# A modulation row computed with the weight tile as the stationary operand

## The reference

```
mod = silu(c) @ mod_w[i] + mod_b[i]          # c: (1, 2048), mod_w[i]: (2048, 12288)
sh_m, sc_m, g_m, sh_f, sc_f, g_f = split(mod, 6)
h = rmsnorm(x, norm_mix_g[i]) * (1 + sc_m) + sh_m
q = h @ w_in[:, 0:1024]; ...                 # the first products of layer 0
```

## Time and profile before

| | us |
|---|---|
| runs, median (3 runs) | 2393.55 (2393.1 to 2397.02) |
| profiled execution | 2393.17 |
| its span, first to last instruction | 2391.2 |
| TensorE busy | 2308.2 (97%) |
| DVE busy | 1847.2 (77%) |
| ACT busy | 1096.9 (46%) |
| mean granted TensorE clock | 0.982 |

### The profile page before, as it was taken

The page is one execution under the profiler, slowest core; times in us unless marked ns, Lnnn a source line. Parts: engine busy times, 40 slices in busy tenths (PEclk is TensorE's granted clock), DMA queues, the critical chain, the costliest instruction groups (busy, mean ns, idle before and its releaser), DMA issues.

```text
span 2391.2 us, 26862 instructions
## 1 busy us (share of the span) xinstructions
PE 2308.2 (97%) x10800; PEld 1870.2 (78%) x10800; DVE 1847.2 (77%) x1748; ACT 1096.9 (46%) x1192; POOL 126.6 (5%) x145
## 2 busy tenths in 40 slices
PE   5999999999999999999998999999999999999998
PEld 2478887778887888878887788877887888878886
DVE  5868997887998888888888777887777556564565
ACT  2244443544554354533554555435555345444454
POOL 0021740010000000000000000000000000000000
PEclk8999999999999999999999999999999999999999
DMA  9958789787997998889889475696776555555554
GB/s 363 383 198 293 250 300 351 250 315 268 348 325 275 359 336 304 291 303 370 323 281 330 130 224 187 253 340 218 274 270 223 193 194 178 190 177 193 193 180 154
DMA packets 259807, 632.89 MB, mean 265 GB/s; under 512 B 23505, under 2 KB 32745, under 8 KB 233978
## 3 DMA queue, kind: packets, MB, share of 16 engines
q1 hardware_dynamic: 258050, 625.90, 73.8%
q10 hardware_dynamic: 1656, 5.60, 0.6%
HBM read 629.36 MB, written 2.10 MB: 264 GB/s over the span
## 4 chain that ended last, share of the span: by engine, by line
PE 80%; DVE 8%; DMA 5%; issue 3%; ACT 2%; SPq 1%; POOL 1%; DVEq 0%; POOLq 0%; ACTq 0%
PE gm L1911 22%; PE gm L1912 22%; PE gm L1918 22%; PE tp L1954 2%; PE gm L1903 2%; DMA mods<-in_mod_w_dram 2%; PE gm L1905 2%; PE gm L1904 2%; DVE w_lo L1213 1%; DVE acc L1230 1%; DVE conv L1659 1%; DMA raw<-in_ffn_w_down_dram 1%; ACT w_hi L764 1%; PE ms L2064 1%; DMA raw<-in_gla_w_in_dram 1%
## 5 line engine op out<-in xcount | busy, mean ns | idle before, releaser
L1213 DVE TENSOR_TENSOR w_lo<-raw,w_hi 128x2048 fp32r<-128x2048 f32 (+1 forms) x378 | 851.9, 2255 | 330.2 <-ACT w_hi L764 328.5
L764 ACT ACTIVATE w_hi<-raw 128x2048 fp32r<-128x2048 f32 (+1 forms) x378 | 703.8, 1864 | 695.5 <-DMA raw<-in_ffn_w_up_dram 242.2
L1911 PE MATMUL gm<-w_hi,h_hi 128*128 128x512 f32 x1816 | 720.7, 397 | 1.6 <-DVE h_lo L1327 1.6
L1912 PE MATMUL gm<-w_hi,h_lo 128*128 128x512 f32 x1816 | 708.1, 390 | 0.0
L1918 PE MATMUL gm<-w_lo,h_hi 128*128 128x512 f32 x1816 | 448.7, 389 | 0.0
L1230 DVE SCALAR_TENSOR_TENSOR acc<-mods,c_col,acc 128x2048 f32<-128x2048 f32 x180 | 422.7, 2349 | 5.3 <-DMA mods<-in_mod_w_dram 4.8
L1911 PEld LDWEIGHTS gm<-w_hi,h_hi 128*128 128x128 f32 x1816 | 341.2, 188 | 77.9 <-issue 4.7
L1918 PEld LDWEIGHTS gm<-w_lo,h_hi 128*128 128x128 f32 x1816 | 340.9, 188 | 70.7
L1912 PEld LDWEIGHTS gm<-w_hi,h_lo 128*128 128x128 f32 x1816 | 341.3, 188 | 69.9 <-issue 1.7
L1911 PE MATMUL gm<-w_hi,a_hi 128*128 128x512 f32 x692 | 275.1, 398 | 11.6 <-DVE a_lo L1682 8.1
L1912 PE MATMUL gm<-w_hi,a_lo 128*128 128x512 f32 x692 | 271.2, 392 | 0.0
(11 more groups left out here) (267 smaller groups left out, 2155.0 us busy)
## 6 DMA issues: line engine op xcount, KB each, us to landing
raw<-in_ffn_w_up_dram SPq DMA_DIRECT2D x176, 1024.0 KB, 5.1
mods<-in_mod_w_dram SPq DMA_DIRECT2D x170, 1024.0 KB, 7.1
raw<-in_ffn_w_down_dram SPq DMA_DIRECT2D x64, 1024.0 KB, 5.1
raw<-in_gla_w_in_dram SPq DMA_DIRECT2D x48, 1024.0 KB, 5.2
mods<-in_kv_mod_w_dram SPq DMA_DIRECT2D x32, 1024.0 KB, 7.0
raw<-in_ffn_w_down_dram SPq DMA_DIRECT2D x32, 768.0 KB, 4.4
raw<-in_gla_w_o_dram SPq DMA_DIRECT2D x16, 1024.0 KB, 7.1
raw<-in_mla_w_o_dram SPq DMA_DIRECT2D x16, 1024.0 KB, 5.6
```

What stands on the lines that cost most here:

```text
L764: act.activation(w_hi[:, k % RAW, 0:words], raw[:, k % RAW, 0:words], ACT.Copy).then_inc(hi_made, 1)
L1213: dve.tensor_tensor(w_lo[:, k % RAW, 0:words], raw[:, k % RAW, 0:words], w_hi[:, k % RAW, 0:words].bitcast(F32), ALU.subtract).then_inc(lo ...
L1911: pe.matmul(o, hi_s[:, kt, tok], wh[:, j, :], start=kt == 0, stop=False)
L1912: pe.matmul(o, lo_s[:, kt, tok], wh[:, j, :], start=False, stop=False)
```

## The change

The tiles of scale that go to TensorE become the stationary operand, one 128x128 block at a time, and c the moving one, a single column. A tile takes 16 such matmuls in place of 4. The result comes out as columns, and adds up in PSUM in the same columns as the sums over `acc`: columns 0 to 3 of `ms` are shift, 4 to 7 scale. A matmul of the identity with the bias columns opens the group (`pre_bias`), so the bias is in it too. A round now needs one fill of `ms` in place of three. DVE's add of the row (L1477), its memset in round 3 and the sums over `acc` for scale in round 3 are gone; it copies the columns out and forms the gain. The copies of the parameters (`pcol`) stand ahead of DVE's second tile in round 0, since `pre_bias` waits for them.

```diff
-        ("pre", 1, 0, 0, 0, 12),
+        ("pre", 1, 0, 0, 0, 4),
...
-                for kind in range(2):
-                    tile_, bias = mod_bias(kind)
-                    bias = pcol[:, tile_, bias + 4 * q:bias + 4 * q + 4]
-                    dve.wait_ge(ms_done, made(fill + kind))
-                    dst = ab[:, col + 1, cols] if kind == 0 else modc[:, 0, cols]
-                    dve.tensor_tensor(dst, ms[:, (fill + kind) % 2, 0:4], bias, ALU.add).then_inc(ms_free, 1)
-                    dve.wait_ge(ms_free, fill + kind + 1)
+                dve.wait_ge(ms_done, made(fill))
+                step.mark(dve.tensor_copy(ab[:, col + 1, cols], ms[:, fill % 2, 0:4]))
+                dve.tensor_copy(modc[:, 0, cols], ms[:, fill % 2, 4:8]).then_inc(ms_free, 1)
+                step.wait(step.base + step.n)
+                dve.wait_ge(ms_free, fill + 1)
...
-                row = acc[0:1, 1, q * W:(q + 1) * W]
-                dve.tensor_tensor(row, row, ms[0:1, (a["pre"].ms + 3 * q) % 2, :], ALU.add).then_inc(ms_free, 1)
...
+            def pre_bias(q):
+
+                if q == 0:
+                    pe.wait_ge(tp_free, 2)
+                tile_, col = mod_bias(0)
+                bias = pcol[:, tile_, col:col + 2 * KT].rearrange("p (g k) -> p g k", g=2)[:, :, 4 * q:4 * q + 4]
+                o = ms_open(a["pre"].ms + q)[:, 0:8].rearrange("p (g k) -> p g k", g=2)
+                pe.matmul(o, ident[:, :], bias, start=True, stop=False)
+
+            def pre_tile(m):
+
+                q, i, kind = PRE_TILES[m]
                 pe.wait_ge(pre_in[PRE_SLOT[m]], pre_landed(m))
-                if i == 0:
-                    pe.wait_ge(tp_free, 1)
-                o, tile_ = ms_open(a["pre"].ms + 3 * q), pre_slot(m)
+                o, tile_ = ms[:, (a["pre"].ms + q) % 2, :], pre_slot(m)
                 for j in range(KT_ITEM):
                     kt = KT_ITEM * i + j
-                    ins = pe.matmul(o[0:1, :], c_col[:, kt:kt + 1], tile_[:, j, :], start=kt == 0,
-                                    stop=kt == (4 if q == 3 else 3) * KT_ITEM - 1)
+                    for b in range(4):
+                        k = 4 * kind + b
+                        ins = pe.matmul(o[:, k:k + 1], tile_[:, j, b * P:(b + 1) * P], c_col[:, kt:kt + 1],
+                                        start=False, stop=False)
                 ins.then_inc(pre_pe, 1)
...
+            def pre_sums(q):
+
+                o = ms[:, (a["pre"].ms + q) % 2, :]
+                for kind in range(2 if q < 3 else 1):
+                    pe.wait_ge(pre_dve, 5 * q + 4 + kind)
                     for b in range(4):
-                        c0 = q * W + b * P
-                        ins = pe.matmul(o[:, b:b + 1], acc[:, kind, c0:c0 + P], ones[:, 0:1],
-                                        start=True, stop=True)
-                    ins.then_inc(ms_done, 1)
+                        c0, k = q * W + b * P, 4 * kind + b
+                        last = k == (7 if q < 3 else 3)
+                        ins = pe.matmul(o[:, k:k + 1], acc[:, kind, c0:c0 + P], ones[:, 0:1], start=False, stop=last)
+                ins.then_inc(ms_done, 1)
```

More of the change, by code:

```diff
@@ L295, in yoco_kernel @@
     TURNED = (3, 6, 7, 8, 9)
-    REDUCE = {0: ("pre", 10), 1: ("pre", 11), 2: ("mod_v", 0), 3: ("mod_r", 0), 4: ("mod_gla", 0),
+    REDUCE = {0: ("pre", 3), 1: ("pre", 3), 2: ("mod_v", 0), 3: ("mod_r", 0), 4: ("mod_gla", 0),
               5: ("modu00", 0), 6: ("modd00", 0), 7: ("modu01", 0), 8: ("modd01", 0), 9: ("modu02", 0),
@@ L519, in made @@
         def made(fill):
-            rows = min(4, (fill - at["pre"].ms + 2) // 3)
-            return fill + 1 - rows - (fill > at["gate"].ms) - (fill > at["latent"].ms)
+            return fill + 1 - (fill > at["gate"].ms) - (fill > at["latent"].ms)
         @block.sync
@@ L1434, in pre_columns @@
             def pre_columns(q):
-                fill, cols = a["pre"].ms + 3 * q + 1, slice(4 * q, 4 * q + 4)
+                fill, cols = a["pre"].ms + q, slice(4 * q, 4 * q + 4)
                 col = A_OF["mix0"]
-                for kind in range(2):
-                    tile_, bias = mod_bias(kind)
-                    bias = pcol[:, tile_, bias + 4 * q:bias + 4 * q + 4]
-                    dve.wait_ge(ms_done, made(fill + kind))
-                    dst = ab[:, col + 1, cols] if kind == 0 else modc[:, 0, cols]
-                    dve.tensor_tensor(dst, ms[:, (fill + kind) % 2, 0:4], bias, ALU.add).then_inc(ms_free, 1)
-                    dve.wait_ge(ms_free, fill + kind + 1)
+                dve.wait_ge(ms_done, made(fill))
[3 more added lines that the diff above has]
+                dve.wait_ge(ms_free, fill + 1)
                 dve.scalar_tensor_tensor(ab[:, col, cols], modc[:, 0, cols], 1.0,
@@ L1457, in _ @@
                 for i in range(4):
-                    gather_pre(8 * q + 2 * i)
                     if q == 0 and i == 1:
@@ L1464, in _ @@
                         dve.wait_ge(tp_free, 2)
+                    gather_pre(8 * q + 2 * i)
+                    if q == 0 and i == 1:
                         normalised("norm0", x_sb, xn)
-                    if i == 0 and q == 3:
-                        step.link(dve.memset(acc[:, 1, q * W:(q + 1) * W], 0.0))
                     if i >= 2 and q < 3:
@@ L2052, in section @@
                 body(1, last=True)
-            def pre_scale(q, i):
-                m = 8 * q + 2 * i + 1
+            def pre_bias(q):
[5 more added lines that the diff above has]
+                pe.matmul(o, ident[:, :], bias, start=True, stop=False)
@@ L2096, in _ @@
             for q in range(4):
-                pre_scale(q, 0)
+                pre_bias(q)
+                pre_tile(8 * q + 1)
                 if q:
                     q_item(q - 1, 0)
-                pre_scale(q, 1)
+                pre_tile(8 * q + 3)
                 pre_turn(q)
-                pre_scale(q, 2)
+                pre_tile(8 * q + 5)
                 if 0 < q < 3:
@@ L2105, in _ @@
                 if q == 3:
-                    pre_scale(q, 3)
-                pre_reduce(q)
+                    pre_tile(8 * q + 7)
+                pre_sums(q)
                 if q == 3:
```

## The result

| | before, us | after, us |
|---|---|---|
| median of 5 runs each | 2393.1 (2388.21 to 2397.02) | 2414.27 (2409.43 to 2419.58) |
| span of the profiled execution | 2391.2 | 2412.3 |
| mean granted TensorE clock | 0.982 | 0.975 |

The changed kernel takes 1.0082 times as long, 95% interval 1.0068 to 1.0097. By the medians it is 21 us slower, where 28.9 were forecast, and lies inside the range of 2408 to 2432.

A forecast was written before the change was run, and what follows sets the result against it. TensorE was taken to bound the opening, full from 75.59 us on but for 1.64 us; rounds adding 7.1 + 8.9 + 12.9 = +28.9 us on 2393.17 gave 2422 us, range 2408 to 2432 (own range 2415 to 2431).

The forecast's parts named there:

- The exchange is even at one clock: TensorE's scale tiles: 32 one-column passes take 3.5 us at full clock, same as before, and 7.1 at the low clock.
- One-column work does not hold the clock: TensorE's opening: clock falls after 3.5 us of one-column passes though busy, and returns 4.4 us into dense work.
- rival A: One-column passes hold the clock, so no change in effect: -1.8 us, 2391.5 us; chance 0.10.
- round 1: Opening, second of four rounds: tiles and items slower by 10.4 us, less 3.3 of waiting for DVE: +7.1 us.
- round 2: Opening, third of four rounds: two items +2.2 each, tile-transposes-tile +4.5, sums and first tile 0: +8.9 us.
- round 3 to the gate: Opening's last round: start +0.5, two items +2.2 each, tile, transposes and two tiles +8.0: +12.9 us.
- The runs of tiles and transposes: Rounds 1 to 3: tile, transposes, tile from 8.0 to 12.5 us; with two last tiles, 11.5 to 19.5.
- The six items: Dense matmuls after one-column work in rounds 1 to 3: each loses 2.2 us, half of 4.4 until the clock rises.
- The work between the sums and a round's first item: Bias and first tile after the sums, rounds 1, 2 and 3: +1.5, 0 and +0.5 us.
- The hold of the clock: One-column work on TensorE runs 3.5 us at 2.4 GHz, the mean of two cases, then 1.2 GHz for the rest.
- Rival B: Milder: clock falls only in long runs, or so late that single tiles escape; 2403 to 2413 us; chance 0.10.
- Rival C: Worse: items between are too short to bring the clock back; some +60 us, 2453 us; chance 0.05.

The follow-up runs named there:

- wide64: The changed kernel with 64 moving columns in place of one in the opening's tile and sum passes, bias matmul 512 columns wide; 2390.55 us, ratio 0.9982.
- wide16: The changed kernel with 16 moving columns in place of one in the opening's tile and sum passes; 2411.13 us, ratio 1.0073.
- few_after: The changed kernel with one of the 16 matmuls of each of TensorE's scale tiles, the rest left out; 2387.22 us, ratio 0.9974.
- few_before: The kernel before the change with one of the 4 matmuls of each of TensorE's scale tiles, the rest left out; 2387.89 us, ratio 0.9981.
- wide64_dvebias: Against wide64: no bias matmul, DVE adds the bias in its two copies, the first tile matmul opens the group; 2390.26 us, ratio 0.9988.

## Why the prediction was right

**The exchange is even at one clock.** Right. Full clock: 3.5 us a tile, forecast 3.5 (61.57 to 65.06). Low clock: 6.7 to 6.8 (66.69 to 73.37, 142.45 to 149.28), forecast 7.1.

**One-column work does not hold the clock.** Right, and shown: with the same instructions, loads and order, the width of the moving operand alone takes the loss away (wide64) or leaves it (wide16). The Trainium skill ("TensorE: Matmul & The Clock Gate", HAM oscillation) ties the loss of the clock to gaps in which TensorE idles. That rule, on which rival A was built, is not enough for this kernel: the clock was 0.50 for 15.20 us in which TensorE was busy throughout. Rival A's sum was -1.8; with the clock held, wide64 measures 0.9982 (0.997 to 0.9994), some -4 us, which doesn't exclude it. The same page of the Trainium skill (LDWEIGHTS) gives a load's time by its columns alone. The trace agrees at full clock, 0.11 us a pass, and not at the low one: 32 passes in 6.7 us are 0.21 each.

**The terms.** From sums' end to sums' end, forecast and measured:

| | forecast | measured |
|---|---|---|
| round 1 | +7.1 | +5.8 (77.4 to 83.2) |
| round 2 | +8.9 | +7.5 (26.9 to 34.4) |
| round 3 to the gate | +12.9 | +10.5 (40.7 to 51.2) |
| sum | +28.9 | +23.9 |
| given back behind the gate | 0 | -2.8 |
| span | +28.9 | +21.1 |

The mechanism was right and the sizes were about a fifth too high. The 5.0 us of the difference spread over three terms.

- The runs of tiles and transposes, 1.8 us. Tile, transposes, tile: forecast 12.5 us, measured 11.8 (61.57 to 73.37) and 12.0 (95.97 to 108.01). Tile, transposes, two tiles: 19.5 forecast, 19.0 measured (130.27 to 149.28). The low-clock pass was taken from 8 passes with their wait, 0.22, where 32 in a row take 0.21. And the transposes were counted at twice their 1.0 us, where they take 1.6 to 1.7 (65.06 to 66.69).
- The six items, 1.7 us. 2.2 us more for each was forecast; against 5.6 before they took 7.6, 8.1, 7.4, 7.9, 7.3 and 6.9, so 1.9 on average. The clock came back 2.9 to 5.5 us into them, by where their matmuls move closer, on average about as late as the 4.4 us taken. But half of the time to its rise was counted as lost, and an item's matmuls start 0.43 us apart at the low clock and 0.23 at the full one, which loses a little less than half.
- The work between the sums and a round's first item, 1.3 us. Forecast +1.5, 0 and +0.5, measured +1.0, -0.4 and +0.1. In round 1 the first of its tiles ended at 53.93, not 54.5.

The hold of the clock was taken as 3.5 us. Four windows that begin with one-column work at full clock and end at the low one give it, by their mean clock, as 4.2, 3.3, 3.8 and 3.2 us, and the two windows around 65 us above as about 3.6:

```profile
81.49:88.30 6.81, 6.81 (x51) 6.75 (x49) 3.56 (x9) 4.02 (x7) 0.00 (x0) 0.81 1.03 379
95.97:101.00 5.03, 5.03 (x40) 5.03 (x39) 4.92 (x6) 0.00 (x0) 0.00 (x0) 0.83 1.06 393
115.92:123.00 7.08, 7.08 (x52) 7.02 (x50) 3.79 (x10) 4.67 (x6) 0.00 (x0) 0.77 0.83 289
130.27:135.00 4.73, 4.73 (x38) 4.73 (x37) 4.45 (x7) 0.00 (x0) 0.00 (x0) 0.84 0.42 70
```

That it fits so well is in part luck. It was the mean of two cases, and in the second of them, at 1313.15, TensorE idled for the last 0.8 us before the fall.

**What was costed at nothing or nearly so.** Right as far as it can be seen: the bias, the copies and the moved parameter copies show nothing in few_after against few_before. The row add is gone and the columns of round 0 come at 47.20 instead of 48.09, which nobody uses, since the next item waits for the tile (53.93).

**What was left out.** The -2.8 us behind the gate. The forecast had the shift pass through unchanged; in fact shorter waits gave back 2.7 of it ahead of 464 us. Behind that, falls of the clock at other places in the two profiles moved the shift by some us either way, and that they cancel at the end is luck. The five runs of the changed kernel differ by 10 us, those of before by 9.

Rival B (a fall in the long runs only, 2403 to 2413) touches the measured runs at their lower end, but not its mechanism: the single tiles at 83.41 and 117.84 lost the clock too. Rival C did not occur: every item brought the clock back within itself.

## What to carry to other kernels

Before a matrix-vector product is turned so that the weights are stationary, ask what its passes move: at one clock 128x128 loads with a single column cost the same as 512 columns moved, but long runs of them lost TensorE's clock though it was busy throughout, and the dense work behind paid for it. Where such passes can't be avoided, try repeating the moving column: 64 columns took no longer here and held the clock, but for places behind a wait. Judge a stretch by the granted clock in it, not by TensorE's busy time.

## What the runs showed of the hardware

- The pass of a 128x128 f32 load takes the same with 1, 32 and 64 moving columns (3.63, 3.67 and 3.68 us for 32 passes at full clock, tail and all), 0.11 us at full clock and 0.21 at the low one.
- Passes of 64 columns kept a high clock over 18.80 us without a gap (wide64_dvebias). It was at the low level behind such work and a wait of 0.87 us (wide64, 121.17) or 1.66 us (wide64_dvebias, 80.89), and stayed high over one of 0.80 (wide64, 80.45).
- They did not bring a low clock back at once: in wide64 the tiles at 14.71, 21.43 and 30.40 took 6.93, 7.03 and 7.09 us, and the one at 48.22, right behind a bias matmul of 512 columns, 4.28.
- With 32 columns the same kernel ran between 2395.58 and 2418.91 us.
- Matmuls that add into columns of one PSUM bank can share one group that its first matmul opens: wide64_dvebias adds eight results of 64 columns after one start.
